# Contracting stages of an encoder trunk: the last weight slab, not the last two, is taken output by output

## What is computed

```python
def squared_relu_mlp(h, w1, w2):
    return jnp.square(jax.nn.relu(h @ w1)) @ w2

for layer in range(DEPTH):                       # DEPTH = 2
...
    x = layer_norm(ALPHA * x + (1.0 + gate) * y, ln_g[layer, 0], ln_b[layer, 0])
...
    h = x * (1.0 + scale) + shift
    y = squared_relu_mlp(h, mlp_w1[layer], mlp_w2[layer])
    x = layer_norm(ALPHA * x + (1.0 + gate) * y, ln_g[layer, 1], ln_b[layer, 1])
```

## Time and profile before

| what | value |
|---|---|
| median of three runs | 2724.23 us (2723.56 to 2727.06) |
| the profiled execution, its own time | 2723.2 us |
| span of that execution, first to last instruction | 2721.4 us |
| PE busy | 2491.4 us, 92% of the span |
| DVE, ACT busy | 67%, 44% |
| mean granted clock of PE | 0.955 of full speed |

### The profile page before, as it was taken

One profiled execution on the slowest core, in us unless ns is written; L12 is line 12 of the kernel. 1 busy time (PEld: TensorE's weight loads), 2 busy tenths in 40 slices (PEclk: granted clock), 3 DMA queues, 4 the chain that ended last, 5 costly groups with the idle time before them and its releaser, 6 DMA issues.

```text
span 2721.4 us, 41210 instructions
## 1 busy us (share of the span) xinstructions
PE 2491.4 (92%) x16196; PEld 2016.3 (74%) x16196; DVE 1823.5 (67%) x1914; ACT 1187.3 (44%) x1050; POOL 111.5 (4%) x154
## 2 busy tenths in 40 slices
PE   5779999976798999999999975699999999999997
PEld 2458888833686888888888751488788888888885
DVE  6976666678756776776767659767756666544444
ACT  4643333354535333334343356634543333443434
POOL 1021000001002000000000011000020000000000
PEclk9889999987798999999999987799999999999998
DMA  9997888722463888888888729588667777555551
GB/s 290 400 336 263 282 277 283 247 70 94 149 208 123 280 283 277 282 281 290 293 284 294 282 101 241 213 279 279 208 202 234 237 237 232 185 197 188 198 188 47
DMA packets 228972, 635.12 MB, mean 233 GB/s; under 512 B 33186, under 2 KB 34852, under 8 KB 208132
## 3 DMA queue, kind: packets, MB, share of 16 engines
q1 hardware_dynamic: 216164, 579.27, 63.4%
q0 software_dynamic: 9536, 34.48, 3.9%
q10 hardware_dynamic: 3168, 19.92, 1.8%
HBM read 613.83 MB, written 19.79 MB: 233 GB/s over the span
## 4 chain that ended last, share of the span: by engine, by line
PE 78%; DVE 15%; ACT 4%; issue 2%; DMA 1%; SPq 0%; DVEq 0%; ACTq 0%
PE PS L293 32%; PE PS L325 26%; PE PS L297 16%; DVE raw L1626 2%; DVE Pb L2079 2%; DVE acc L2074 1%; ACT Pb L1147 1%; DVE X L1698 1%; DMA araw<-in_ada_w 1%; DVE raw L1630 1%; PE PS L1070 1%; PE PS L1045 1%; DVE WF L1630 1%; ACT H L1147 1%; DVE wlo L288 0%
## 5 line engine op out<-in xcount | busy, mean ns | idle before, releaser
L288 DVE TENSOR_TENSOR wlo<-raw,whi 128x2048 fp32r<-128x2048 f32 x368 | 844.1, 2294 | 698.0 <-ACT whi L284 697.0
L284 ACT ACTIVATE whi<-raw 128x2048 fp32r<-128x2048 f32 x368 | 705.0, 1917 | 1212.7 <-PE PS L293 787.7
L293 PE MATMUL PS<-H,whi 128*128 128x512 f32 x3840 | 1214.0, 397 | 19.1 <-DVE wlo L288 9.6
L297 PEld LDWEIGHTS PS<-H,wlo 128*128 128x128 f32 x3840 | 724.4, 189 | 170.8
L297 PE MATMUL PS<-H,wlo 128*128 128x256 f32 x3840 | 756.7, 279 | 0.0
L325 PE MATMUL PS<-whi,H 128*128 128x512 f32 x2048 | 637.5, 391 | 10.0 <-DVE H L1746 10.0
L293 PEld LDWEIGHTS PS<-H,whi 128*128 128x128 f32 x3840 | 588.0, 189 | 23.9 <-issue 13.0
L325 PEld LDWEIGHTS PS<-whi,H 128*128 128x128 f32 x2048 | 386.6, 189 | 93.6 <-DVE wlo L288 11.1
L325 PE MATMUL PS<-wlo,H 128*128 128x512 f32 x1024 | 400.1, 391 | 0.0
L185 DVE SCALAR_TENSOR_TENSOR acc<-araw,cact,acc 128x1024 f32<-128x1024 f32 x240 | 307.9, 1283 | 1.2 <-DMA araw<-in_ada_w 0.8
L325 PEld LDWEIGHTS PS<-wlo,H 128*128 128x128 f32 x1024 | 193.4, 189 | 39.8
(11 more groups left out here) (314 smaller groups left out, 1502.6 us busy)
## 6 DMA issues: line engine op xcount, KB each, us to landing
raw<-in_mlp_w SPq DMA_DIRECT2D x256, 1024.0 KB, 6.1
araw<-in_ada_w SPq DMA_DIRECT2D x274, 512.0 KB, 4.8
raw<-in_mix_w_in SPq DMA_DIRECT2D x64, 1024.0 KB, 7.6
raw<-in_s_w_glu SPq DMA_DIRECT2D x32, 1024.0 KB, 7.3
acc<-in_ada_w SPq DMA_DIRECT2D x40, 512.0 KB, 8.1
raw<-in_ada_w POOLq DMA_DIRECT2D x32, 512.0 KB, 4.2
raw<-in_mix_w_out SPq DMA_DIRECT2D x16, 1024.0 KB, 5.1
vmat<-Pb ACTq DMA_DIRECT2D x8, 1024.0 KB, 8.4
```

The source lines that it names most:

```text
L284: nc.scalar.activation(whi[:, s % 2, :], raw[:, s, :], ACT.Copy).then_inc(S("hi_done"), 1)
L288: nc.vector.tensor_tensor(wlo[:, s % 2, :], raw[:, s, :], whi[:, s % 2, :].bitcast(F), ALU.subtract).then_inc(S("lo_done"), 1)
L293: return nc.tensor.matmul(PS[:, b, :], w, H2[:, :, k, :], start=first, stop=last, skip_group_check=True)
L297: return nc.tensor.matmul(PS[:, b, 0:T], w, H2[:, 0, k, :], start=False, stop=last, skip_group_check=True)
```

## The change

In both contracting stages, slab 2 of the last body becomes an ordinary slab: PE waits for it alone and makes its 24 products, three into each bank. Then PE waits for slab 3, and only slab 3 goes output by output, with three products for each bank in place of six. The number of products, copies, transposes and additions is the same; no load is added, removed or moved; the streams of ACT, DVE, POOL and SP are untouched. Slab 2's `slab_used` is signalled by its own last product instead of the one before the last three.

```diff
-                for sl in range(2):
+                for sl in range(3):
                     down_slab(s, n, 7, sl)
-                for sl in range(2, 4):
-                    down_ready(s, n, 7, sl)
+                down_ready(s, n, 7, 3)
...
                 for m in range(3):
-                    for sl in range(2, 4):
-                        for t in range(2):
-                            last = down_products(sl, 2 * m + t)
+                    for t in range(2):
+                        last = down_products(3, 2 * m + t)
                     last.then_inc(S("tile_full"), 1)
                     if m:
                         back(m - 1)
                 for t in range(2):
-                    last = down_products(2, 6 + t)
-                    if t:
-                        last.then_inc(S("slab_used"), 1)
                     down_products(3, 6 + t).then_inc(S("slab_used" if t else "tile_full"), 1)
                     if t == 0:
                         back(2)
```

## The result

The changed kernel takes 2709.51 us (median of six runs, 2704.12 to 2716.05); the kernel before took 2725.7 us beside it (six runs, 2723.56 to 2730.17). The ratio is 0.994, 95% interval 0.9926 to 0.9954: faster by 0.5 to 0.7%. The profiled execution of the changed kernel is the fastest of its six, 2704.12 us with a span of 2702.3 us. Of the 35 runs of the kernel before beside the first experiments, one took 3593.84 us at a granted clock of 0.647; it is left out, and their median, 2726.23 us, is that of the other 34.

A forecast was written before the change was run, and what follows sets the result against it. PE, 78% of the path, idled for slab 3 in each contracting stage, then ran at lower clock. Hole (9.82 us) plus clock (4.55) gave 14.37 us off, forecast 2709.8 us, range 2707 to 2714.

The forecast's parts named there:

- The hole: PE's wait for slab 3 ahead of ready slab 2 disappears in both contracting stages: -4.91 us each, -9.82 in all.
- The clock: Slow products behind the wait return to full clock: -2.49 us in layer 1, -2.06 in layer 0, together -4.55.
- rival that only the idleness is won: The clock falls elsewhere, in layer norms and final transposes, giving back all 4.55 us: 2714.4 us; chance 0.10.
- The drain: Slab 3's output-by-output end of each stage, in pieces half as long, still overlaps across ACT, DVE and PE: cost 0.
- two near misses: In the drain, ACT's first copy has 0.09 us to spare and DVE's additions barely finish in time: some 0.2 us per layer.
- rival of pieces in series: Copy, transposes and additions no longer fit under the next piece's products: +10.5 us a layer, 2731 us; chance 0.02.
- The clock in the drain: Rival: transposes between pieces of six products lower the clock, 7.1 us per layer: 2724 us, or 2717 from half-way; chance 0.04.
- What follows: Behind both stages everything dependent moves along, so gains of 6.97 us (layer 0) and 7.40 (layer 1) reach the end.

The follow-up runs named there:

- the late slab 3: Changed kernel with DVE multiplying half of X, or both halves, by 1.0 behind the last split, and PE waiting for it before slab 3: 2710.89 and 2716.58 us.
- the new order with the old wait: Changed kernel's order of products, but PE waits for both slabs ahead of slab 2: 2724.56 us against 2726.23 for the kernel before, ratio 0.9999.
- The filled hole: Kernel before, with 11 zero-weight products into bank 7 ahead of the wait for slabs 2 and 3, both layers: 2721.44 us against 2724.3, ratio 0.9984.
- the first filling: Kernel before, with 19 zero-weight products into bank 7 ahead of the wait for slabs 2 and 3, both layers: 2729.38 us, ratio 1.0021.

## Why the prediction was right

The forecast was 2709.8 us; measured were 2709.51 and, again, 2708.75. That the first is only 0.3 us off is luck in part. The forecast starts from a median of 2724.23, and beside the changed kernel the kernel before had 2725.7; the change was forecast at 14.4 us, and by medians it is 16.2 and 15.6. The mechanism is borne out by the stages, term by term.

**The hole.** Its removal was put at 4.91 us in each layer, with slab 2's 24 products (5.44 us) as the cover and 0.53 us to spare. The stretches measured 5.44 us and no wait follows. That the cover is what does it is shown by the late slab 3, where 0.52 to 0.53 us of each delay are covered and the rest is a hole, and by the new order with the old wait, which shows no gain.

**The clock.** The term was 4.55 us, between bounds of 0 and 4.55. The filled hole measured it alone: 4.3 us by the stages, 1.9 to 6.8 by the kernel's time. The rival that only the idleness is won, 2714.4 us, has the loss come back outside the stages, so the whole times decide it: a gain of 9.8 us lies below both intervals of the whole change, 12.5 to 20.2 and 10.1 to 17.4. That a smaller part comes back outside is not excluded.

The Trainium skill (TensorE: Matmul & The Clock Gate, Part 1) has the number of slow products differ from run to run. The stages bear this out: with the hole they took 21.44, 21.58, 21.89, 22.21, 22.32 and 22.41 us, six cases in four profiles; without it 14.86 to 14.89, six cases in four profiles. But the draw is not the whole of it: the three cases of layer 0 (21.44 to 21.89) all lie below the three of layer 1 (22.21 to 22.41), and no run shows why.

**The drain.** It was costed at 0 and counted out at 9.48 us; it took 9.45 and 9.44. The two near misses, ACT's first copy and DVE's eight additions in a row, both came out on the right side. The rival of pieces in series falls with it.

**The clock in the drain.** It stayed at 1.00 with eight transposes between pieces of six and three products. The statement of the Trainium skill (TensorE: Matmul & The Clock Gate, Part 4: PE-mode transpose) that the full clock does not engage for transposes, which spoke for that rival, is not borne out here: a group of eight took 1.03 us, as before, where the final eight took 1.78 at a granted clock of 0.57. In the changed kernel the final 32, with no product among them, ran at 1.00 as well (2690.02 to 2695.50). What no run shows is whether transposes alone would raise the clock.

**What follows.** Layer 0's gain reaching the end was argued from the chain; the kernel with layer 0 alone shows it, 2.7 to 8.4 us. The sum 14.37 us stands against 14.44 in the profile's two stages. The 4 us between the stages in the profiled execution, the fastest of six, are not in the sum, and their cause stays open.

No version that came out of the experiments beats the changed kernel: what is left in the stage is the 0.25 us ahead of the last transposes, below what a measurement can tell.

## What to carry to other kernels

When an engine waits for two things and has work for the first, put the work ahead of the second wait: here the rows showed a ready slab of 5.4 us of products behind a wait of 4.9. On PE, price a hole at its length and also at the products behind it that run at the lower clock, here 1.7 to 2.6 us for each hole of 4.9. And before an output-by-output drain is shortened to half pieces, add up copy, transposes and additions for each piece against the next piece's products: it was free here, with 0.1 us to spare by the prediction's count.

## What the runs showed of the hardware beyond that

A product of plain 32-bit floats, 128x128 by 128x256, took 0.42 us and two records at a granted clock of 1.00 (19 of them: 38 records, 8.0 us), while the rounded type takes 0.2267 us for 512 columns. I had read a record as a product, and so the first filling was twice too long.

DVE multiplied 128x2048 floats by a constant in place in 1.22 us, while the subtraction of two such tensors (L288) takes 2.29 us. The Trainium skill (VectorE: DVE Perf Modes, Mode 2×_2P) says that a one-source operation between SBUF operands can in this mode move two elements per cycle and one with two sources can't; the two times agree with that.

A hole of 2.79 us on PE was followed by a stretch at a granted clock of 0.57 (a mean of the two levels); behind holes of 0.46 and 1.59 us in layer 1 and of 1.66 us in layer 0 the stages grew by no more than 0.12 us beyond the delay itself.
